# Constant products on TensorE between the stages of a two-block transformer kernel, and the rotary cosines on GpSimd

## The reference, cut to what matters

```python
def rmsnorm(x, g):                      # over features, and over each head of q and k
    y = x * lax.rsqrt(jnp.mean(x * x, axis=-1, keepdims=True) + NORM_EPS)
    return y * g

def rope_1d(x, pos):                    # rotary position: x cos + rotated(x) sin
    ang = pos[:, None] * inv[None, :]
    cos, sin = jnp.cos(ang)[None, :, None, :], jnp.sin(ang)[None, :, None, :]
    x1, x2 = x[..., :half], x[..., half:]
    return jnp.concatenate([x1 * cos - x2 * sin, x2 * cos + x1 * sin], axis=-1)

def compress(kx, pos, w1, w2):          # nsa: 31 windows of 32 tokens
    blocks = kx[:, idx] + pos
    hid = jax.nn.gelu(jnp.einsum('bnld,ldm->bnm', blocks, w1))
    return hid @ w2
```

## Time and profile before

| | |
|---|---|
| median of 3 runs | 3607.36 us (3605.43 to 3614.57) |
| profiled execution: its time, its span | 3606.53 us, 3604.7 us |
| busy: PE, DVE, ACT, POOL | 2890.3, 1519.9, 926.1, 343.3 us |
| mean granted TensorE clock | 0.878 of full speed |

### The profile page before, as it was taken

One profiled execution on the slowest core, in us unless ns is written; L12 is line 12 of the kernel. 1 busy time (PEld: TensorE's weight loads), 2 busy tenths in 40 slices (PEclk: granted clock), 3 DMA queues, 4 the chain that ended last, 5 costly groups with the idle time before them and its releaser, 6 DMA issues.

```text
span 3604.7 us, 55490 instructions
## 1 busy us (share of the span) xinstructions
PE 2890.3 (80%) x22870; PEld 1958.2 (54%) x22870; DVE 1519.9 (42%) x2840; ACT 926.1 (26%) x1634; POOL 343.3 (10%) x475
## 2 busy tenths in 40 slices
PE   6848897799969879866888748789984888878995
PEld 5625555677756336752777616644433635564442
DVE  2263453444442364246777563411114374442112
ACT  1223332322231125203222212211113216431111
POOL 0010000000010000001444200011101010011111
PEclk8957698999989779985999969899996869988997
DMA  3214362222221000010000111089982100016995
GB/s 141 92 52 142 127 234 94 82 82 93 93 76 36 15 1 1 24 50 1 4 4 4 55 57 52 38 309 337 339 305 82 62 1 1 1 75 231 342 337 198
DMA packets 63482, 384.75 MB, mean 107 GB/s; under 512 B 7824, under 2 KB 7840, under 8 KB 26896
## 3 DMA queue, kind: packets, MB, share of 16 engines
q1 hardware_dynamic: 41792, 292.60, 22.2%
q0 software_dynamic: 21456, 88.82, 6.7%
HBM read 344.65 MB, written 36.70 MB: 106 GB/s over the span
## 4 chain that ended last, share of the span: by engine, by line
PE 68%; DVE 14%; issue 5%; DVEq 4%; ACT 4%; DMA 2%; ACTq 1%; POOL 0%; POOLq 0%; PEldq 0%; PEld 0%
PE psum L324 14%; PE psum L467 10%; PE psum L2622 10%; PE psum L2642 5%; PE psum L1805 3%; PE psum L1534 3%; PE psum L2302 2%; PE psum L1051 2%; PE psum L1032 2%; PE psum L2609 2%; PE psum L1453 2%; PE psum L872 1%; PE psum L1042 1%; PE psum L847 1%; DVE stat L1113 1%
## 5 line engine op out<-in xcount | busy, mean ns | idle before, releaser
L324 PE MATMUL psum<-arena_r 128*128 128x512 f32 (+1 forms) x928 | 325.1, 369 | 94.3 <-DVE weight_slots_r L361 90.0
L2622 PE MATMUL psum<-weight_slots,arena 128*128 128x512 f32 x800 | 359.1, 602 | 2.4 <-ACT arena L2664 2.4
L324 PE MATMUL psum<-h_t_r,arena_r 128*128 128x512 f32 (+1 forms) x736 | 274.5, 373 | 12.6 <-DVE weight_slots_r L361 12.3
L324 PE MATMUL psum<-arena_r,weight_slots_r 128*128 128x512 f32 (+1 forms) x768 | 279.3, 364 | 0.0
L467 PE MATMUL psum<-arena_r 128*128 128x512 f32 x704 | 252.0, 399 | 28.9 <-DVE weight_slots_r L551 15.8
L324 PEld LDWEIGHTS psum<-arena_r 128*128 128x128 f32 x928 | 177.9, 196 | 135.4 <-issue 108.4
L2622 PEld LDWEIGHTS psum<-weight_slots,arena 128*128 128x128 f32 x800 | 149.5, 192 | 176.0 <-issue 170.6
L467 PE MATMUL psum<-arena_r,weight_slots_r 128*128 128x512 f32 x528 | 208.7, 395 | 0.0
L1805 PE MATMUL psum<-x_t 64*64 64x64 f32 x5376 | 181.6, 221 | 30.3 <-DVEq L1986 14.9
L1805 PEld LDWEIGHTS psum<-x_t 64*64 64x64 f32 x5376 | 167.8, 136 | 41.9 <-DVEq L1986 19.7
L2642 PE MATMUL psum<-weight_slots,arena 128*128 128x512 f32 x400 | 180.2, 593 | 1.6 <-issue 1.6
(11 more groups left out here) (395 smaller groups left out, 4932.7 us busy)
## 6 DMA issues: line engine op xcount, KB each, us to landing
weight_slots<-in_weights SPq DMA_DIRECT2D x277, 1024.0 KB, 6.0
y_rows<-arena POOLq DMA_DIRECT2D x50, 512.0 KB, 8.5
h_rows<-arena POOLq DMA_DIRECT2D x10, 512.0 KB, 3.1
x_keep<-x_t POOLq DMA_DIRECT2D x1, 3072.0 KB, 14.2
x_t<-x_keep POOLq DMA_DIRECT2D x1, 3072.0 KB, 16.2
x_t<-in_x POOLq DMA_DIRECT2D x1, 2048.0 KB, 9.7
arena<-in_cmp_w POOLq DMA_DIRECT2D x1, 2048.0 KB, 7.8
out_x<-x_t SPq DMA_DIRECT2D x1, 2048.0 KB, 7.2
```

The lines of the kernel that those rows point to most:

```text
L324: last = self.nc.tensor.matmul(self.bank(n), w[:, kt, :], x[:, kt, a:b], start=(i == 0), stop=(i == len(passes) - 1))
L2622: last = nc.tensor.matmul(ps[t % 2], self.xt[:, t % 2, kt * P:(kt + 1) * P], w[:, k, :], start=(kt == 0), stop=(kt == KT - 1))
```

## The change

Such a product is float32, 128 rows by 128 columns, 128 columns wide. It waits for nothing of its own, but stands in TensorE's order. The calls:

```diff
 Norm.tensor        pe.drain().then_inc(self.sums[0], 1)
+    self.kern.warm(self.kern.ps[1], self.WARM_ROOT)                        # 8
     pe.wait_ge(self.inverses[0], self.inverses[1] + 1)
     ...            pe.drain().then_inc(self.spread[0], 1)
+    self.kern.warm(self.kern.ps[1], self.WARM_END if self.tiles == KT else 0)   # 20
 Split
+    def tensor(self, pe): self.kern.warm(self.kern.ps[7], 16)
 HeadNorm.tensor
+    kern.warm(kern.ps[7], 4)
     for n, (g, j, x, _) in enumerate(self.units):
         pe.wait_ge(s, base + n // 2 + 1)
         ...matmul(kern.ps[g][at:at + 32, 0:w], ...).then_inc(self.sum[0], 1)
+        kern.warm(kern.ps[7], 1)
+    kern.warm(kern.ps[7], 16)
     for n, (g, j, x, _) in enumerate(self.units):
         ...spreading products
+    kern.warm(kern.ps[0], 12)
 Rope.tensor
+    self.kern.warm(self.kern.ps[7], 4)
     for n, x in enumerate(self.units):
         ...matmul(self.kern.ps[n % 4][0:self.d, :], self.rot_t, x, ...).then_inc(self.rot[0], 1)
+        self.kern.warm(self.kern.ps[7], 1)
 FoxGates
+    def tensor(self, pe): self.kern.warm(self.kern.ps[7], 20)
 Compress.tensor
+    self.kern.warm(self.kern.ps[7], 16)
     for j in (0, 1):
         for l in range(CMP_LEN):
             last = t.matmul(...)
+            if l % 8 == 7: self.kern.warm(self.kern.ps[7], 2)
 WkvPrep.tensor
+    self.kern.warm(self.kern.ps[7], 8)
     ...sums
     for i, (kind, c, d, s) in enumerate(self.items):
         ...product, and every third time a spreading product
+        self.kern.warm(self.kern.ps[7 if i < 7 else 5], 1)
 RwkvOut.tensor
         ...the two sums of unit n
+        self.kern.warm(self.kern.ps[7], 4)
         if n:
             variance(n - 1)
+            self.kern.warm(self.kern.ps[7], 4)
```

Rope moves the cosine products to GpSimd, writes the sine products back into PSUM, and runs one unit ahead:

```diff
+    def gpsimd(self, pool):
+        for n, x in enumerate(self.units):
+            if n >= 4:
+                pool.wait_ge(self.done[0], self.done[1] + n - 3)
+            self.nc.gpsimd.tensor_tensor(out=self.straight(n), in0=x, in1=self.cos, op=ALU.mult).then_inc(self.scaled[0], 1)
+
     def vector(self, dve):
         v, d = self.nc.vector, self.d
+        def rotated(n):
+            dve.wait_ge(self.rot[0], self.rot[1] + n + 1)
+            t = self.kern.ps[n % 4][0:d, :]
+            v.tensor_tensor(out=t, in0=t, in1=self.sin, op=ALU.mult)
+            dve.drain()
+
+        rotated(0)
         for n, x in enumerate(self.units):
-            t = self.kern.scratch[0:d, n % 2, :]
-            dve.wait_ge(self.rot[0], self.rot[1] + n + 1)
-            v.tensor_tensor(out=t, in0=self.kern.ps[n % 4][0:d, :], in1=self.sin, op=ALU.mult)
-            v.tensor_tensor(out=x, in0=x, in1=self.cos, op=ALU.mult)
-            dve.drain()
-            v.tensor_tensor(out=x, in0=x, in1=t, op=ALU.add).then_inc(self.done[0], 1)
+            if n + 1 < len(self.units):
+                rotated(n + 1)
+            dve.wait_ge(self.scaled[0], self.scaled[1] + n + 1)
+            v.tensor_tensor(out=x, in0=self.straight(n), in1=self.kern.ps[n % 4][0:d, :], op=ALU.add).then_inc(self.done[0], 1)
```

More of the change, by code:

```diff
@@ L164 @@
     REST_BY_POOL = 5
+    WARM_ROOT, WARM_END = 8, 20
     def __init__(self, k, src, dst, tiles, group, segs, gain, ones, shift=None, parts=None):
@@ L269, in __init__, with tensor @@
         self.rounded = self.count("operand_rounded", tiles)
+    def tensor(self, pe):
+        self.kern.warm(self.kern.ps[7], 16)
     def scalar(self, act):
@@ L788, in __init__, with straight @@
         self.rot = self.count("rope_rotated", len(units))
+        self.scaled = self.count("rope_scaled", len(units))
         self.done = self.count("rope_done", len(units))
+    def straight(self, n):
+        return self.kern.scratch[0:self.d, n % 4, :]
     def tensor(self, pe):
+        self.kern.warm(self.kern.ps[7], 4)
         for n, x in enumerate(self.units):
@@ L1313, in __init__, with tensor @@
         self.stored = self.count("fox_rows_stored", 64)
+    def tensor(self, pe):
+        self.kern.warm(self.kern.ps[7], 20)
     def vector(self, dve):
@@ L1381, in tensor @@
                                 start=(l == 0), stop=(l == CMP_LEN - 1))
+                if l % 8 == 7:
+                    self.kern.warm(self.kern.ps[7], 2)
             last.then_inc(self.p[0], 1)
```

## The result

| | before | after |
|---|---|---|
| median | 3608.36 us (4 runs) | 3694.02 us (4 runs, 3688.59 to 3694.35) |
| ratio, 95% interval | | 1.0232, 1.0214 to 1.0249 |
| profiled execution, its span | 3606.53, 3604.7 us | 3694.03, 3692.2 us |
| mean granted clock | 0.878 | 0.906 |

The direction was forecast, the size was not: +87.5 us on the profiled executions (3694.03 against 3606.53) where +30.7 was forecast, outside the range. TensorE's clock is higher than before and the kernel is slower.

What follows compares the result with a forecast made beforehand. TensorE was taken to bound the kernel, holding 68% of the chain; terms +23, +16.5, +12.8, −21.6, +4, −1, −1, +1 and −3 summed to +30.7 on 3606.53 us, giving 3637 us (+0.8%), range 3607 to 3672.

Steps and rivals of the forecast that it cites:

- The point on which it parted from the change: HeadNorm sums: strip products run side by side, but with a full-width product behind each they must run in a row.
- Rival C: Constant product and strip sum share the array; HeadNorm loses nothing, WkvPrep gains 8 us, Rope 21.6: 3578 us, 10%.
- First HeadNorm: Its 14 sums of 512 columns stay at the half clock, 2.40 us a unit: +23 us.
- rival B: Filler raises the clock where half was assumed: first HeadNorm −16 us, Compress in part −6: 3615 us, 14%.
- Second HeadNorm: Its 16 narrow and 16 wide sums run at the full clock, 0.84 and 1.26 us a unit: +16.5 us.
- Third HeadNorm: Its 4 narrow and 20 wide sums run at the full clock, likewise as in the second: +12.8 us.
- Rival A: Clock falls where full was assumed: second HeadNorm +29, third +25, WkvPrep +34, second Rope +21; one gives about 3664 us, 24%.
- WkvPrep: Full clock taken as kept; pairs that ran at once are undone, eating the clock's gain: −1 us, bounds −1 and +34.
- Compress: Full clock for a few us, then half; products ahead and in eight groups cost more: +4 us, bounds −11 and +10.
- Rope: VectorE's unit falls from 1.97 to 1.36 us, GpSimd and TensorE hidden at the full clock, 36 units: −21.6 us.
- Rival D: In Rope VectorE and GpSimd exclude each other, unit 2.60 us, +45 us: 3682 us, 4%.
- The rest: RwkvOut −1 us, nine Norms +1, TokenProject after the first Norm and the same after Rope −3.

Runs made afterwards that it cites:

- the four variants of rows and columns: Changed kernel, product behind each HeadNorm sum varied: 128 rows by 128 columns 3694.0 us, 128 by 32 3667.7, own rows by 32 3635.0, own rows by 128 3693.1.
- The delay run: Kernel before, with FoxGates setting its row of ones five times instead of once, so everything behind starts about 2 us later: median 3603.5 us, ratio 0.9989.

## Why the prediction was wrong, step by step

**The point on which it parted from the change** (a full product shuts the strips out): right, and shown by the four variants of rows and columns. Rival C, 10%, is out.

**First HeadNorm**, +23 at the half clock: +25.3, at the half clock through all its sums, so rival B did not come. The unit was 2.57 instead of 2.40 us. The term that is off is the change of form, taken as 0.13 us from the earlier trace rows; (2.57 − 1.71 − 0.43) / 2 gives 0.22.

**Second HeadNorm**, +16.5 at the full clock: +21.6 at 0.97. The clock was right; the unit is 1.40 and 0.97 us instead of 1.26 and 0.84. At the full clock a change costs 0.17 us, not 0.10.

**Third HeadNorm**, +12.8: +38.1. This is the step that failed: "likewise", that is the full clock as in the second. The clock was half for 51 of the 76 us, with a unit of 2.57 us instead of the 1.26 of the forecast. The two differ in the rows, 64 against 96, and behind the same 0.66 us wait the one lost the clock and the other did not; that the rows decide is argued from this, not shown by itself. Two products behind each sum held the clock (59.3 us; the wait at that place was then 0.44 us), where one did not. Rival A had priced it, +25 on top; it came with that. (Two small slips stand beside it: 1233.05 + 34.5 is 1267.55, not 1267.2, and 2860.15 + 29.5 is 2889.65, not 2889.3, so both terms were meant to be 0.3 us larger.)

**WkvPrep**, −1 with the bound +34: +32.5. The same failure: after 4.5 us at half the full clock held for 20.5 us, and the remaining 57.7 ran at half, where the forecast had all 32 items at the full clock. "So I take it as kept" rested on the 0.97 of the recurrence, which is other work. I chose the end of the range that was 34 us away from the truth, and gave all of rival A 24% for one step. Its steps are no separate mishaps: in both, work of 64 rows and less with one product between did not hold the full clock, in the HeadNorm behind a wait and in WkvPrep without one. Together the two terms are 25.3 + 33.5 = 58.8 us off, where the whole sum was 56.8 short: the other misses nearly cancel.

**Compress**, +4: +7.1 at 0.59, with the clock full for the first groups and half from about 291 us on, as forecast. A pair of products with its two changes costs 1.15 us at half, where I had 1.11. The full clock lasted for two of the eight groups and a part of the third, until 291 us, and gave back under 4 us, where I had 5 (estimated from 1.90 and 3.55 us for a group of 16 records at either level). A group at half takes 3.55 us, where the old rows give 26.66 / 8 = 3.33.

**Rope**, −21.6: −19.7. The first −9.4 at 1.37 us a unit; the second −10.3, since TensorE's 1.42 us is over VectorE's 1.36. Rival D is out: VectorE kept its 1.37 us a unit while GpSimd was busy for 20.01 of the stage's 24.30 us. I had TensorE's at 1.26 with the small change of form. Of the three VectorE operations of a unit before, the sum, too, read two SBUF operands, not the moved one alone; the new sum reads one of them from PSUM.

**The rest**, −3: −2.4. TokenProject gave 0.9 instead of 3, RwkvOut 0.7, the Norms −0.9 to +1.2 each.

**Attention**, no term: −15.0. It hid part of the error; with Attention as before the kernel would have been at about 3709. Nothing in the profile before told that the stage has lengths 15 us apart. The delay run shows that it needs no constant product. In 13 profiled executions, the one before among them, it took 266 to 270 us four times and 249 to 255 nine times, by how long it ran at the half clock; in two of the nine short ones products stood in its waits, in the other eleven executions nothing in it was changed.

## What to carry to other kernels

Before putting a product on TensorE to keep its clock, look at what it stands between: small products in strips or in other rows run side by side, and one full product among them costs all of that. Products with the rows and the column strip of the work around them do not cost that, but here they brought nothing either: 28.5, 40.4 and 36.9 us against 28.0, 40.4 and 36.5 with none. Two places paid: products of 128 rows and 32 columns among 96-row sums (36.9 instead of 40.4 us), and products in the waits (WkvPrep 41.6 instead of 49.5). Price a chain at both clock levels: the same one ran at either, by how it began, and could lose the full one behind a wait or without. A mean clock that rises is no gain in itself: it went from 0.878 to 0.906, and the kernel took 86 us more.

## What the hardware showed that I had not expected

- A change of form costs more between 64 or 96 rows by 32 columns and 128 by 128 than between the two forms of the earlier trace rows: 0.22 us at the half clock and 0.17 at the full one, against 0.13 and 0.10. It costs the same 0.22 between 64 by 32 and 64 by 128, and (2.40 − 1.71 − 0.43) / 2 = 0.13 between 64 by 32 and 128 by 32.
- 96-row and 128-row products run beside each other in different strips (36.9 us for a whole HeadNorm), 64-row and 128-row ones do not (51.2). Among 96-row sums in strips, a product of 128 rows and 32 columns kept the clock full through all of the second HeadNorm in four kernels (36.9 us each), one of 96 rows and 32 columns in one trace did not (40.4).
- A chain of identical units (64-row sum, 128 by 128 product) ran at 1.39 us a unit through one stage and at 2.56 through the same stage of another kernel. In the third HeadNorm the fall came within 2 us behind a wait of 0.66 us, in two kernels at different distances from the stage's start, and more than 45 us of unbroken work did not lift the clock back.
- The same instructions took 249 to 270 us in Attention, 135 to 142 in the first PairAttention and, without any constant product, 36 to 50 in WkvPrep, by when the granted clock rose and fell in them. It may be why the kernel before spreads over 3590 to 3618 us; only one of those executions has a trace. What decides it in a given execution stays open: with the work shifted by 2.6 us, one execution of eleven came under 3600.
